# Ordering the high-weight and low-weight products inside one weight unit of a split-precision transformer kernel

## The reference, cut to what matters

```python
proj = h @ w_in                                   # 256 x 2048 by 2048 x 4096
return x + jnp.concatenate([y_pool, y_mem], axis=-1) @ w_out
u = jnp.einsum('bsd,df->bsf', h, w_up[l])         # 2048 x 5632
x = x + jnp.einsum('bsf,fd->bsd', jax.nn.silu(g) * u, w_down[l])
```

## Time and profile before

| what | value |
|---|---|
| runs | 2038.60, 2039.43, 2040.60 us (median 2039.43) |
| span of the profiled execution | 2037.8 us; the runs lie 0.8 to 2.8 us above it |
| TensorE matmul busy | 2019.6 us, 99% |
| TensorE weight loads busy | 1763.8 us, 87% |
| VectorE (DVE) busy | 1452.9 us, 71% |
| ScalarE (ACT) busy | 1036.3 us, 51% |
| GpSimd (POOL) busy | 415.8 us, 20% |
| mean granted TensorE clock | 0.996 |

### The profile page before, as it was taken

One profiled execution on the slowest core, in us unless ns is written; L12 is line 12 of the kernel. 1 busy time (PEld: TensorE's weight loads), 2 busy tenths in 40 slices (PEclk: granted clock), 3 DMA queues, 4 the chain that ended last, 5 costly groups with the idle time before them and its releaser, 6 DMA issues.

```text
span 2037.8 us, 29295 instructions
## 1 busy us (share of the span) xinstructions
PE 2019.6 (99%) x11506; PEld 1763.8 (87%) x11506; DVE 1452.9 (71%) x2056; ACT 1036.3 (51%) x1548; POOL 415.8 (20%) x376
## 2 busy tenths in 40 slices
PE   8999999999999999999999999999999999999998
PEld 7888888888888888888878888888888888888887
DVE  6866788788796556876656678777776567777755
ACT  6744544566433554644555555455454344545443
POOL 0014553300000344430122235211010000101122
PEclk9999999999999999999999999999999999999999
DMA  9664556567654334555444445555556655555664
GB/s 339 218 193 151 193 186 196 184 226 239 210 182 145 114 114 135 187 203 189 152 161 141 154 149 190 183 191 190 190 190 187 190 191 190 192 191 192 183 189 145
DMA packets 104809, 374.22 MB, mean 184 GB/s; under 512 B 11840, under 2 KB 13152, under 8 KB 104288
## 3 DMA queue, kind: packets, MB, share of 16 engines
q1 hardware_dynamic: 104384, 371.83, 54.8%
q10 hardware_dynamic: 288, 0.52, 0.1%
HBM read 370.21 MB, written 2.10 MB: 183 GB/s over the span
## 4 chain that ended last, share of the span: by engine, by line
PE 94%; DVE 3%; DMA 1%; ACT 1%; POOL 0%; issue 0%; DVEq 0%; SPq 0%; ACTq 0%
PE psg L554 50%; PE psg L555 26%; PE psg L621 2%; PE psg L623 2%; PE psg L622 2%; PE psg L595 1%; PE pst L595 1%; DVE s_w L1726 1%; PE pst L752 1%; PE psg L598 1%; PE pst L598 1%; PE pss L843 1%; PE pst L660 1%; DMA s_stage<-in_mk 1%; PE pso L863 1%; ACT s_w L1156 0%
## 5 line engine op out<-in xcount | busy, mean ns | idle before, releaser
L1726 DVE TENSOR_TENSOR s_w<-s_stage,s_w 128x1024 fp32r<-128x1024 f32 (+3 forms) x698 | 861.4, 1236 | 350.8 <-ACT s_w L1156 348.0
L1156 ACT ACTIVATE s_w<-s_stage 128x1024 fp32r<-128x1024 f32 (+3 forms) x698 | 727.0, 1043 | 730.6 <-PE psg L555 633.6
L554 PE MATMUL psg<-s_ry,s_w 128*128 128x512 f32 x2560 | 900.4, 394 | 1.8 <-DVE s_qc L1780 1.8
L555 PE MATMUL psg<-s_ry,s_w 128*128 128x256 f32 x2560 | 723.2, 283 | 0.0
L554 PEld LDWEIGHTS psg<-s_ry,s_w 128*128 128x128 f32 x2560 | 482.5, 188 | 108.0 <-issue 2.3
L555 PEld LDWEIGHTS psg<-s_ry,s_w 128*128 128x128 f32 x2560 | 485.8, 190 | 0.4
L554 PE MATMUL psg<-s_rh,s_w 128*128 128x512 f32 x1216 | 428.0, 394 | 0.3 <-DVE s_w L1726 0.3
L555 PE MATMUL psg<-s_rh,s_w 128*128 128x256 f32 x1216 | 342.7, 282 | 0.0
L554 PEld LDWEIGHTS psg<-s_rh,s_w 128*128 128x128 f32 x1216 | 228.3, 188 | 49.0 <-issue 1.0
L554 PE MATMUL psg<-s_hid,s_w 128*128 128x512 f32 x704 | 244.1, 390 | 0.0
L555 PEld LDWEIGHTS psg<-s_rh,s_w 128*128 128x128 f32 x1216 | 229.8, 189 | 0.7
(11 more groups left out here) (417 smaller groups left out, 2203.4 us busy)
## 6 DMA issues: line engine op xcount, KB each, us to landing
s_stage<-in_wo SPq DMA_DIRECT2D x96, 512.0 KB, 3.6
s_stage<-in_wg SPq DMA_DIRECT2D x84, 512.0 KB, 3.5
s_stage<-in_wu SPq DMA_DIRECT2D x84, 512.0 KB, 3.9
s_stage<-in_ain SPq DMA_DIRECT2D x64, 512.0 KB, 3.7
s_stage<-in_wd SPq DMA_DIRECT2D x64, 448.0 KB, 3.3
s_stage<-in_wkv SPq DMA_DIRECT2D x32, 512.0 KB, 3.6
s_stage<-in_wd SPq DMA_DIRECT2D x32, 512.0 KB, 3.4
s_stage<-in_bq SPq DMA_DIRECT2D x24, 512.0 KB, 3.6
```

The lines of the kernel that those rows point to most:

```text
L554: e.matmul(o, M.WH[:, r, ws], xx, start=begin, stop=False)
L555: m = e.matmul(o[:, T:2 * T], M.WL[:, r, ws], xh, start=False, stop=end)
L1156: e.activation(M.weights(c, 0, n, shift), M.staged(c, n), ACT.Copy).then_inc(S["wh"], 1)
L1726: e.tensor_tensor(M.weights(c, 1, n, shift), M.staged(c, n), M.weights(c, 0, n, shift), ALU.subtract).then_inc(S["wl"], 1)
```

## The change

Inside `b_unit`, the loop over the blocks of a unit becomes two loops: first the H matmul of every block, then the L matmul of every block. The wait for the low weights moves between the two; ahead of the first loop stands a wait for the high weights alone.

```diff
         if c:
+            w.wait_ge("wh", c + 1)
+        for kk in range(nk):
+            ready(k0 + kk)
+            e.matmul(o, M.WH[:, r, kk * mw:kk * mw + mw], x(k0 + kk)[1], start=first and kk == 0, stop=False)
+        if c:
             w.wait_ge("wl", c + 1)
         for kk in range(nk):
-            ws = slice(kk * mw, kk * mw + mw)
-            ready(k0 + kk)
-            xh, xx, _ = x(k0 + kk)
-            begin, end = first and kk == 0, last and kk == nk - 1
-            e.matmul(o, M.WH[:, r, ws], xx, start=begin, stop=False)
-            m = e.matmul(o[:, T:2 * T], M.WL[:, r, ws], xh, start=False, stop=end)
+            m = e.matmul(o[:, T:2 * T], M.WL[:, r, kk * mw:kk * mw + mw], x(k0 + kk)[0], start=False, stop=last and kk == nk - 1)
         m.then_inc(S["units"], 1)
```

## The result

Four executions of each kernel gave medians of 2052.3 us after (2051.1 to 2054.0) and 2039.0 us before (2037.1 to 2040.6). The ratio is 1.007, 95% interval 1.0057 to 1.0082. The profiled execution of the changed kernel spans 2049.3 us, against 2037.8.

What follows compares the result with a forecast made beforehand. Matmul pitch on TensorE was taken as the bound: 7.4 us gained in the units less 2.0 us after side products gave 5.4 us, 2039.4 to 2034.0 us. Its own range was 2031 to 2037 (chance 0.40), with rivals 2027 to 2048.

Steps and rivals of the forecast that it cites:

- What bounds the kernel: TensorE's matmuls, busy 99% of the span; only how closely they follow each other could change, 4.5 us per nanosecond per couple.
- Waits: Before a unit's H and L runs: at most 0.3 us gained; the earlier `ready` of block 7 taken as zero, at most 4 us.
- The L run: A unit's L matmuls in a row: 116.7 ns each as in the pool product, against 118.3, load hidden.
- The H run: A unit's H matmuls in a row: 226.7 ns each as in the pairs, against 228.3 in the alternating order.
- the pairs: Trace rows of 512-column matmuls moving one segment, from 31.98 to 37.42 us: 226.7 ns, the pitch taken for H.
- the gates: Trace rows of 512-column matmuls moving the same operand as H: 233 ns, set aside because their 72-column blocks start at changing addresses.
- Changing over: First H after an L run, once per unit: 8.3 ns more; last H and last L keep 228.3 and 118.3 ns.
- Units after a side product: 101 of 568 units whose first H does not follow an L: 20 ns more each, 2.0 us lost.
- B: H run never settles, two segments, unshifted weights: 233 ns per H, 24 ns more per unit, 2053 us; chance 0.24.
- A: Order makes no difference, or change-overs cost another 10 ns per unit: 2036 to 2042 us; chance 0.25.
- C: Runs settle at once, changing over costs nothing: 14.9 us gained less 2 us, 2026.5 us; chance 0.10.
- D: Eight L in a row run into their weight loads, pitch 0.19 us: 278 us lost; chance 0.01.

Runs made afterwards that it cites:

- the bench: TensorE alone at the real kernel's addresses, constant data, other engines idle: H run 233.4 ns a matmul, L run 116.7, high-then-low unit 2.800 us from the second on.
- run 1: Not a follow-up run: the words come from "the L run 1 ns shorter than forecast", where 1 ns is the amount by which the L run was shorter.
- 8, 8: Kernel before, alternating order, high and low weights of the tiles both 8 values further into their slots: 2057.7 us, ratio 1.0096.

## Why the prediction was wrong, point by point

- **What bounds the kernel: right.** The pitch alone decided; the waits of TensorE and the release of the slots are as before.
- **Waits: right**, and shown by the kernel with one wait. No tile matmul waits for an activation, so the earlier `ready` costs nothing.
- **The L run: right.** 116.7 ns, in the kernel and in the bench; the load of 128 x 128 weights stays hidden under it.
- **The H run: the step that failed.** The prediction took 226.7 ns from the pairs over the 233 ns of the gates, on the ground that the gates' blocks start at changing addresses. It measured 233 ns, 233.4 in the bench. The addresses were indeed what mattered, but I had them on the wrong side: the pairs' row is the one that does not carry over to the tiles, as their addresses stand. The gates' row, which moves the same operand, was the row to take, though no run shows that the gates and the pairs have their pitches from this same cause: their own addresses were never moved. By the step's own sum the H run was to be 1.823 us and was 1.866, 43 ns more. With the L run 1 ns shorter than forecast and the waits as before, the plain units came out 27 ns longer and not 13 shorter: 40 x 403 = 16.1 us, and 39 x 64 = 2.5 us for the units of 7. Less 1.6 us, by which the 101 units and the rest came out shorter than forecast, that is the distance of 16.9 us between the forecast span of 2032.4 and the measured 2049.3.
- **Changing over: too small.** I took 8.3 ns for the first H alone. With the high weights 8 further, where settled H take 226.7 ns, a run of eight H had 1.848 us and not 1.823: 34 ns above eight settled ones, spread over five H at the start and one at the end. The unit took 2.780 us and not 2.760, so even a settled pitch of 226.7 would have brought no gain, as that kernel shows (1.0004).
- **Units after a side product: not what the sum had.** I took 20 ns more for each of the 101 on top of the plain unit's gain of 13, 7 ns longer in all. Their median was 21 ns longer, less than the 27 ns of a plain unit; their sum was 0.5 us less, by the clock as said above. The lower clock level in one execution and not in the other was no term of the prediction.
- **Rivals.** B was right, with 24 ns a unit worked out and 27 measured, and an H run of 1.87 us where it had 1.86; I gave it 0.24. That its 2053 us is so near the 2052.3 is in part luck, since it took the 24 ns for all 568 units and the 101 behind other work added nothing to the measured sum. Its mechanism was half right: an H run at these addresses is slow however long it is, but not because of the two segments. A, C and D are out. The rule of the Trainium skill cited under A (TensorE: Matmul & The Clock Gate, "Back-to-back issue gap"), a fixed 2.5 ns above the columns divided by 2.4 GHz, which the section gives for a matmul in isolation, would have given no change: here the same 512 columns took 226.6 to 234 ns a matmul in settled runs of H, by the distance between two addresses.

What stays open is why the distance matters. The runs show only that the pitch depends on where the weights lie against the moving operand with no other engine at work, and that there is more than one repeating pattern. That the load of the next weights and the moving stream get in each other's way is not shown: the load by itself, without a moving stream, was not timed. Nor is it shown why an H among L takes 228.3 ns at the same addresses at which an H among H takes 233.3.

## What to carry to other kernels

When matmuls stand back to back, read their pitch, not their busy time, and compare it with rows that have the same moving operand and the same addresses, before those that only have the same shape. A change of order changes which load runs beside which stream; try it together with shifts of the operands by a few values, which here were worth more (23 us less) than the order (13 us more). A bench that runs TensorE alone at the kernel's addresses gives unit lengths that most units of the kernel then had (2.773, 2.780, 2.746 and 2.720 us), but not always: at 8, 8 it gave 2.826, and a quarter of the plain units took 2.773. Test several ways into the pattern. And compare the stretches at the lower clock level before reading a difference of a microsecond between two spans.

## What the runs showed of the hardware that was not expected

- With float32r operands, the settled pitch of a 512-column matmul with its own 128 x 128 load runs from 226.6 to 234 ns with the distance between the two operands in memory; a step of 16 bytes can be the difference (233.3 to 226.6). A 256-column one took 116.7 ns in the plain L run and 113.3 in the fastest alternating pattern, and up to 120 at other shifts (0.960 us for eight).
- The alternating couple had most often 346.7, 350 or 353 ns, and at few pairs of shifts 340 (units of 2.773, 2.800, 2.827 or 2.720 us); values between them occur too. Which one is taken can depend on one delay of 0.3 us long before.
- At the lower clock level the extra time is gone. In the kernel before, the granted clock fell to 0.50, its lower level of 1.2 GHz, while TensorE ran 48 matmuls of 15 columns (622.75 to 628.87 us). In the stretch behind them a couple took 630.30 - 629.66 = 0.64 us: 768 columns at 1.2 GHz with nothing added. At 2.4 GHz 768 columns are 320 ns, and the best couple took 340. The windows view (busy, granted clock, DMA share, GB/s) and the timeline of that stretch:

```profile
629.00:633.00 4.00, 4.00 (x14) 0.50 0.04 16
640.00:644.00 4.00, 4.00 (x27) 1.00 0.52 175
```

```profile
629.66 0.63 PE L554 MATMUL psg<-s_ry,s_w 128*128 128x512 f32 x1
630.08 0.41 PE L555 MATMUL psg<-s_ry,s_w 128*128 128x256 f32 x1
630.30 0.63 PE L554 MATMUL psg<-s_ry,s_w 128*128 128x512 f32 x1
```
